# Two transformer blocks on one core: the first block's attention placed between its projection units, and the order in which the split halves of the weights are made

## The chip, the cores and the metric

The kernel runs on one core of one Trainium2 chip. The metric is the device time of one execution in microseconds (us), as the median of three runs. TensorE (PE) multiplies, with its weight loads shown apart as PEld; VectorE (DVE), ScalarE (ACT), GpSimd (POOL) and SyncE (SP) are the other engines. Each of them works through its own list of instructions in order and waits on semaphores for the others.

## The reference, cut to what matters

There are 256 tokens of width 1024. The first block has two layers, the second block one. Everything is float32.

```python
for i in range(2):                                   # first block
    xn = rms_norm(h, norm_mix[i]);  mn = rms_norm(mem, norm_mem[i])
    mk, mv = split(mn @ w_mem_kv[i])                 # 4 memory heads of 64
    proj = xn @ w_in[i]                              # q, k, v of 12 heads of 64; in layer 0 12 forget
                                                     # gates; and the query of the 4 memory heads
    # layer 0: s = q k / 8 + F[t] - F[s], F = cumsum(log_sigmoid(gate)), causal, softmax, p v
    # layer 1: s = q k / 8 - slope * (t - s),        causal, softmax, p v   (256 tokens: one block)
    # memory heads: softmax(qm mk / 8) mv            over 256 memory rows, no mask
    h = h + concat(heads) @ w_out[i]
    gu = rms_norm(h, norm_ffn[i]) @ w_gate_up[i]     # 2 x 2816 columns
    h = h + (silu(gu[:, :2816]) * gu[:, 2816:]) @ w_down[i]
x = rms_norm(h, norm_final)
mod = silu(c) @ w_ada + b_ada                        # 6 x 1024 values, used in the second block
# second block: a latent attention of 8 heads, a gated linear recurrence, and a layer of 16384 experts
# of which each token takes 128 rows of expert_u and 128 of expert_v
```

## The kernel before, in words

**Weights.** The dense weights are a stream of units of 128 x 1024 floats (512 KB). SP loads them two at a time into a ring of six units. One unit is what TensorE needs for one output tile of 128 columns over the whole depth of 1024 (or for half of a 256-column value tile, or for one row block of `w_down`).

**Split products.** In the first block each matmul is made of three products in a faster number format: every operand is split into a high half (rounded) and a low half (the rest), and high x high, low x high and high x low are added. For each unit u, ScalarE copies the raw unit to its high half (`split_hi`, L771), VectorE subtracts it to get the low half (`split_lo`, L1067), and TensorE then runs 8 + 8 + 8 matmuls (`split_T`, L413, L418 and L422; `pair_S`, L449; `down`, L552, L556 and L557). There are three buffers for split units, so the split of unit u waits until unit u-2 has begun on TensorE (`split_begun`). `units_begun` counts the low halves done; TensorE waits for it before the low product, and in `down` before the first product.

**A layer.** In the order of the stream: memory keys (2 units), memory values (2), in layer 0 the forget gates (1), then q (6 units), k (6), v (6), memory queries (2), then the whole attention, then `w_out` (8 units), then the feed-forward (66 units). So layer 0 has 33 units before its feed-forward and layer 1 has 32. Norms are sums of squares by a matmul with ones (L462), a square root on ScalarE (L761), a reciprocal (L1053) and eight scalings (L1059) on VectorE, and then the split of the normed input chunk by chunk (L784, L1080).

**Attention** (`attention`, one for each engine) has 32 items in each layer, an item being one head and one block of 128 queries, with 128 keys for the first block, and 256 for the second and for memory heads. For an item TensorE makes the scores (L489, and in layer 0 another matmul that subtracts F, L493), VectorE masks (L1100 in layer 0, L1103 in layer 1, a copy L1107 for memory heads) and takes the maximum (L1113), ScalarE takes the exponential and its sum (L802), VectorE inverts the sum (L1118) and scales (L1124), TensorE transposes the probabilities (L503), ScalarE copies them (L812), TensorE multiplies by v (L516), and ScalarE stores the head twice (L819, L820). The transposes and the product with v run three and four items behind the scores. These matmuls are plain float32. During attention no weight unit is used.

**Feed-forward.** The units are g0 u0 g1 u1 d0, then g(f) u(f) d(f-1) for f = 2 to 21, then d21, where g is gate, u is up and d is down. TensorE follows that order. VectorE and ScalarE do not split in step with f: both enter the feed-forward with two units split already (by the loop over `w_out`), and VectorE's loop is, for each f from 2:

```python
split_lo(d(f-1)); split_lo(g(f+1)); product(f); split_lo(u(f+1)); product_lo(f); ada_sum(...)
```

`product` (L1167) is silu(gate) x up, which waits until TensorE has finished u(f) (`up_ready`). `product_lo` (L1174) is the low half of it. `ada_sum` (L1152, L1155) is one of the 48 rows of `mod`, whose weights POOL loads into two buffers. One is done for each f in both feed-forward loops, and the 12 that are left between the q and k units of layer 1, with the angles for the second block's rotary embedding (`trig`).

**The second block** starts at about 820 us. From about 1200 us it is the expert layer, whose rows come by indirect DMA.

## Time and profile before

| what | us |
|---|---|
| median of the three runs (1812.03 to 1815.88) | 1815.13 |
| the profiled execution's own time | 1809.4 |
| its span | 1807.7 |
| PE / DVE / ACT busy in the span | 1595.3 / 1018.7 / 726.1 |
| layer 0: from the first q unit to the end of `w_out` | 49.15 to 225.13 |
| of it attention | 108.38 to 200.72 |
| layer 1: the same | 444.62 to 620.99 |
| of it attention | 517.48 to 595.58 |
| feed-forward of layer 0, from g2 on | 250.90 to 425.94 |

The span runs from the first to the last instruction. Busy time is what an engine's instructions took; a matmul counts as busy at either level of TensorE's clock, so a busy TensorE can still run at half speed. "PEclk" is the granted clock as a share of 2.4 GHz: 0.50 is 1.2 GHz.

### The profile page before, as it was taken

What the parts mean: (1) busy time and instruction counts of PE and PEld (TensorE: products, weight loads), DVE (VectorE), ACT (ScalarE), POOL (GpSimd) and SP (SyncE); (2) the same over time, 40 slices, a digit from 0 to 9 for tenths busy, and PEclk for the clock granted to TensorE, in tenths of its full rate; (3) what the DMA queues carried; (4) which work ended last, traced back from release to release, by engine and by line L of the source; (5) the groups of instructions that cost most, each with busy time, mean ns of one, the idle gap of its engine ahead of it and who ended that gap; (6) DMA issues with size and microseconds to landing.
All of it is one profiled execution on the core that took longest, in us unless ns stands there. A gap on an engine that the chain in (4) does not pass through costs nothing.

```text
span 1807.7 us, 23290 instructions
## 1 busy us (share of the span) xinstructions
PE 1595.3 (88%) x7836; PEld 1144.4 (63%) x7836; DVE 1018.7 (56%) x2272; ACT 726.1 (40%) x1750; POOL 513.4 (28%) x573
## 2 busy tenths in 40 slices
PE   5999999999899899997999997888887778777776
PEld 4975789998865799996888786444442223222222
DVE  4443476666654566663335315666666667666644
ACT  4543354444343444443154201434444444444432
POOL 1000000000100000000000001777777776777773
PEclk9975899999975899998999899999999999999999
DMA  7420247664730256662433233999999999999997
GB/s 282 165 92 1 71 152 254 239 249 152 255 118 1 94 198 244 244 220 76 144 110 119 70 140 118 411 410 409 409 409 409 409 409 409 410 409 409 409 410 285
DMA packets 102017, 443.97 MB, mean 246 GB/s; under 512 B 11376, under 2 KB 11648, under 8 KB 84272
## 3 DMA queue, kind: packets, MB, share of 16 engines
q0 software_dynamic: 81632, 297.80, 42.0%
q1 hardware_dynamic: 19584, 141.57, 21.5%
q10 hardware_dynamic: 720, 3.59, 0.5%
q8 instruction: 43, 0.70, 0.2%
q14 instruction: 38, 0.31, 0.0%
HBM read 441.86 MB, written 1.05 MB: 245 GB/s over the span
## 4 chain that ended last, share of the span: by engine, by line
PE 58%; DMA 22%; POOL 9%; DVE 4%; issue 4%; ACT 2%; ACTq 0%; POOLq 0%; DVEq 0%
DMA late<-expert_v,idx 18%; PE PS L400 12%; PE PS L413 7%; PE PS L418 7%; PE PS L422 7%; POOL attn L348 5%; POOL late L356 5%; PE PS L709 4%; PE PS L516 4%; PE PS L489 3%; PE PS L449 3%; PE PS L552 2%; PE PS L556 2%; PE PS L557 2%; DMA attn<-expert_u,idx 2%
## 5 line engine op out<-in xcount | busy, mean ns | idle before, releaser
L709 PE MATMUL PS<-late,wrg 128*128 128x512 f32 x1024 | 500.2, 616 | 130.6 <-DMA late<-expert_v,idx 114.5
L709 PEld LDWEIGHTS PS<-late,wrg 128*128 128x128 f32 x1024 | 177.5, 190 | 439.1 <-DMA late<-expert_v,idx 276.6
L1545 DVE CUSTOM_DVE_ANT_0 attn<-attn,PS 128x1024 f32<-128x1024 f32 x256 | 312.5, 1221 | 238.3 <-DMA attn<-expert_u,idx 238.3
L348 POOL DMA_INDIRECT attn<-expert_u,idx x256 | 241.4, 943 | 380.8 <-DVE idx L1529 300.5
L356 POOL DMA_INDIRECT late<-expert_v,idx x256 | 241.4, 943 | 98.5 <-PE PS L709 54.3
L334 POOL DMA_DIRECT2D ada<-w_ada x46 | 24.4, 530 | 734.2 <-DVE mod L1155 734.2
L1067 DVE TENSOR_TENSOR early_splits<-ring,early_splits 128x1024 fp32r<-128x1024 f32 x132 | 161.6, 1225 | 98.4 <-ACT early_splits L771 92.3
L771 ACT ACTIVATE early_splits<-ring 128x1024 fp32r<-128x1024 f32 x132 | 139.4, 1057 | 150.6 <-PE PS L413 104.2
L400 PE MATMUL PS<-XN,ring 128*128 128x256 f32 x816 | 183.8, 386 | 15.6 <-DVE XN L1376 7.8
L400 PEld LDWEIGHTS PS<-XN,ring 128*128 128x128 f32 x816 | 158.0, 194 | 42.8 <-DVE XN L1376 8.2
L1013 ACT ACTIVATE gel<-dot 128x1 f32<-128x1 f32 x256 | 51.3, 200 | 283.6 <-DVE dot L1545 283.1
L1067 DVE TENSOR_TENSOR late_split<-ring,late_split 128x1024 fp32r<-128x1024 f32 x65 | 79.6, 1224 | 63.8 <-ACT late_split L771 63.6
L1021 ACT ACTIVATE wrg<-con,wts 128x128 f32<-128x128 f32 x256 | 102.7, 401 | 23.5 <-PE PS L709 0.4
L413 PE MATMUL PS<-x_split,early_splits 128*128 128x256 f32 x600 | 92.3, 297 | 17.4 <-ACT x_split L784 10.0
L771 ACT ACTIVATE late_split<-ring 128x1024 fp32r<-128x1024 f32 x65 | 68.6, 1056 | 77.9 <-PE PS L413 41.5
L556 PE MATMUL PS<-product_split,early_splits 128*128 128x256 f32 x344 | 97.2, 283 | 0.0
L552 PE MATMUL PS<-product_split,early_splits 128*128 128x256 f32 x344 | 96.9, 282 | 0.4 <-DVE early_splits L1067 0.4
L557 PE MATMUL PS<-product_split,early_splits 128*128 128x256 f32 x344 | 96.8, 281 | 0.0
L413 PEld LDWEIGHTS PS<-x_split,early_splits 128*128 128x128 f32 x600 | 82.0, 198 | 21.8 <-issue 18.3
L418 PE MATMUL PS<-x_split,early_splits 128*128 128x256 f32 x600 | 88.2, 292 | 0.0
L422 PE MATMUL PS<-x_split,early_splits 128*128 128x256 f32 x600 | 87.2, 290 | 0.0
L418 PEld LDWEIGHTS PS<-x_split,early_splits 128*128 128x128 f32 x600 | 81.2, 201 | 0.2 <-DVE early_splits L1067 0.2
(245 smaller groups left out, 2341.8 us busy)
## 6 DMA issues: line engine op xcount, KB each, us to landing
ring<-wstream SPq DMA_DIRECT2D x134, 1024.0 KB, 4.8
ada<-w_ada POOLq DMA_DIRECT2D x48, 512.0 KB, 3.9
attn<-expert_u,idx POOLq DMA_INDIRECT x256, 17.7
late<-expert_v,idx POOLq DMA_INDIRECT x256, 17.7
con<-const ACTq DMA_DIRECT2D x1, 1168.0 KB, 11.9
MEM<-mem_t ACTq DMA_DIRECT2D x1, 1024.0 KB, 7.7
X<-x_t ACTq DMA_DIRECT2D x1, 1024.0 KB, 9.6
subk<-sub_keys POOLq DMA_DIRECT2D x1, 1024.0 KB, 7.5
```

The costliest lines, as they stand in the source:

```text
L348: gp.indirect_dma_start(UB[i % SLOTS_U], None, expert_u, bass.IndirectOffsetOnAxis(ap=idx[:, n % 3, k:k + 1], axis=0)).then_inc(u_landed[i ...
L356: gp.indirect_dma_start(VB[i % SLOTS_V], None, expert_v, bass.IndirectOffsetOnAxis(ap=idx[:, n % 3, k:k + 1], axis=0)).then_inc(v_landed[i ...
L400: mm = pe.matmul(PS[:, bank, 0:T], w(k), src[:, k, :], start=(k == 0), stop=(k == KC - 1))
L413: mm = pe.matmul(out, hi_of(u)[:, k * P:(k + 1) * P], xh[:, k, :], start=(k == 0), stop=False)
L418: pe.matmul(out, lo_of(u)[:, k * P:(k + 1) * P], xh[:, k, :], start=False, stop=False)
L422: mm = pe.matmul(out, hi_of(u)[:, k * P:(k + 1) * P], xl[:, k, :], start=False, stop=(k == KC - 1))
L552: mm = pe.matmul(out_o, whi, FH[:, par, :], start=first and o % 2 == 0, stop=False, skip_group_check=True)
L556: pe.matmul(out_o, wlo, FH[:, par, :], start=False, stop=False, skip_group_check=True)
L709: mm = pe.matmul(PS[:, 2 * b + g, :], DIAG[:, i % 8, :], VB[i % SLOTS_V][:, g * 512:(g + 1) * 512], start=n % 8 == 0 and k == 0, stop=n % ...
L771: act.activation(hi_of(u), raw(u), ACT.Copy).then_inc(hi_ready, 1)
L1067: ve.tensor_tensor(lo_of(u), raw(u), hi_of(u).bitcast(F32), ALU.subtract).then_inc(units_begun, 1)
L1545: ve.tensor_tensor_reduce(row, row, H2N[n // 8], 1.0, 0.0, ALU.mult, ALU.add, dot[:, n % 2, k:k + 1]).then_inc(dot_ready, 1)
```

## The change

The first block is rebuilt; the second keeps its order. In words:

1. The units of a layer are used in another order: memory queries first, then q, k and v pair by pair. After 16 of the units TensorE does one *group* of attention (two heads of one query block), so that projection units and groups alternate. Three units of `w_out` are begun before the last heads are there, and finished when they are. The raw stream in memory is unchanged: SP loads units one by one (512 KB each) in the new order.
2. Attention works in groups: one maximum, one reciprocal and one copy of the transposed probabilities for two heads, masks and exponentials for each head. Memory heads are not copied: maximum and exponential read the scores where TensorE wrote them. A group's transposes, scores of the next group and product with v are issued at the end of a unit (`attend`).
3. In ScalarE's order `split_hi` of the unit two ahead stands before the exponentials of the group; in VectorE's order `split_lo` stands before the scaling of its probabilities.
4. The norm of x is computed at the start beside that of the memory, and in layer 1 after the first memory unit. `early_table` asks for ScalarE's function tables earlier. After the feed-forward the sums into X start as soon as two columns of `w_down` are done (`down_part`).
5. Both feed-forwards: ScalarE and VectorE start their loop at the first unit that is not split, in another order (below). Two `ada_sum` for each f in layer 0, one for each of the first 12 in layer 1, none between the projections. `trig` moves into the feed-forward of layer 1, and the split of the normed memory for layer 1 to the last two f of layer 0.
6. `w_rg` and `w_ig` are loaded after the second feed-forward.

```diff
+FUSED = (("qm", 0, 0), ("qm", 1, 1), ("q", 0, 1), ("k", 0, 1), ("v", 0, 1), ("v", 1, 0),
+         ("q", 1, 1), ("k", 1, 1), ("q", 2, 1), ("k", 2, 1), ("v", 2, 0), ("v", 3, 0),
+         ("q", 3, 1), ("k", 3, 1), ("q", 4, 1), ("k", 4, 1), ("v", 4, 0), ("v", 5, 0),
+         ("q", 5, 1), ("k", 5, 1), ("wo", 0, 1), ("wo", 1, 1)) + tuple(("wo", c, 0) for c in range(2, KC))
+PAIR_ORDER = (6, 7, 0, 1, 2, 3, 4, 5)
+HELD = 3
...
@@ tensor @@
+            def attend(layer, before, now):
+                if before is not None:
+                    group_turn(layer, before)
+                if now is not None:
+                    group_scores(layer, now)
+                if before is not None:
+                    group_values(layer, before)
...
+                for s, (kind, c, _) in enumerate(FUSED[:-KC]):
+                    u = FUSED_AT[layer] + s
+                    if kind == "v":
+                        pair_half(bank["v", c | 1], u, c % 2, x)
+                    else:
+                        proj(bank[kind, c], u, x, fresh)
...
+                    attend(layer, before, group_at[s])
+                    before = group_at[s]
...
+                for c in range(HELD):
...
+                    out_part(bank["wo", c], u, PAIR_ORDER[:EARLY], first=True, signal=c == 0)
+                    attend(layer, before, group_at[s])
+                    before = group_at[s]
+                pe.wait_ge(heads_lo, base + 14)
+                for c in range(HELD):
+                    out_part(bank["wo", c], out_at + c, PAIR_ORDER[6:7])
+                pe.wait_ge(heads_lo, base + 16)
+                for c in range(HELD):
+                    mm = out_part(bank["wo", c], out_at + c, PAIR_ORDER[7:8], last=True, signal=c > 0)
...
@@ scalar @@
+                for s, (kind, c, _) in enumerate(FUSED[:-KC]):
+                    split_hi(FUSED_AT[layer] + s + 2)
+                    if layer == 0 and s == 0:
+                        forget_gate()
+                    if before is not None:
+                        group_exps(layer, before)
...                 # take(...) of this unit's tile
+                    if before is not None:
+                        group_turned(layer, before)
+                        group_heads(layer, before)
+                    before = group_at[s]
...
             def feed_forward(layer):
-                u = units[0]
-                split_hi(u)
-                split_hi(u + 1)
+                u = LAYER_AT[layer] + PROJ_UNITS[layer]
...
+                split_hi(u + 2)
                 silu(0, 0, False)
+                split_hi(u + 3)
                 product_hi(0, 0, False)
...
+                split_hi(u + 4)
                 silu(1, 1, False)
-                split_hi(u + 4)
                 product_hi(1, 1, False)
                 u += 5
...
@@ vector @@
+                    if before is not None:
+                        group_tops(layer, before)
+                    split_lo(FUSED_AT[layer] + s + 2)
+                    if earlier is not None:
+                        group_low(layer, earlier)
+                    if before is not None:
+                        group_normalise(layer, before)
+                    earlier, before = before, group_at[s]
...
             def feed_forward(layer):
+                def looped(u, i, m):
+                    split_lo(u + 3 * m, i)
+                    split_lo(u + 3 * m + 1, i)
+                    product(i * 2 + (m + 2), m, True)
+                    split_lo(u + 3 * m + 2, i)
+                    product_lo(i * 2 + (m + 2), m, True)
+
-                u = units[0]
-                split_lo(u)
-                split_lo(u + 1)
+                u = LAYER_AT[layer] + PROJ_UNITS[layer]
+                split_lo(u + 2)
                 product(0, 0, False)
+                split_lo(u + 3)
                 product_lo(0, 0, False)
-                split_lo(u + 2)
-                split_lo(u + 3)
...
+                split_lo(u + 4)
                 product(1, 1, False)
-                split_lo(u + 4)
                 product_lo(1, 1, False)
...
                 u += 5
-                with ve.Fori(0, loops) as i:
-                    for m in range(2):
-                        split_lo(u + 3 * m, i)
-                        split_lo(u + 3 * m + 1, i)
-                        product(i * 2 + (m + 2), m, True)
-                        split_lo(u + 3 * m + 2, i)
-                        product_lo(i * 2 + (m + 2), m, True)
-                        ada_sum(j0 + m, m, i, i * 2 + (steps + m))
+                if layer == 0:
+                    with ve.Fori(0, loops) as i:
+                        for m in range(2):
+                            looped(u, i, m)
+                            for a in range(2):
+                                ada_sum(i * 32 + 16 * (m + 1), i * 4 + (steps + 2 * m + a + 1), i * 4 + (2 * m + a), a)
```

Before, `units[0]` is the layer's first feed-forward unit plus two, because two of its units were split already. After the change u is that first unit itself. So in terms of f, the new loop of VectorE (and of ScalarE, with silu in place of product) is:

```python
split_lo(g(f)); split_lo(u(f)); product(f); split_lo(d(f-1)); product_lo(f); ada_sum(...) as said
```

TensorE's feed-forward loop is unchanged: g(f), u(f), d(f-1).

## Rows read from the trace of the kernel before

**Rows 1.** The page: the granted clock in 40 slices of 45 us.
```profile
PEclk9975899999975899998999899999999999999999
```

**Rows 2.** Busy time by stage: stretch, us, busy (count) of PE, PEld, DVE, ACT, POOL; PEclk, DMA share, GB/s.
```profile
22.20:49.15 26.95, 23.59 (x136) 21.68 (x137) 18.67 (x33) 11.80 (x24) 4.99 (x9) 0.84 0.58 223
49.15:108.38 59.23, 57.93 (x485) 57.52 (x483) 26.35 (x24) 30.91 (x44) 0.00 (x0) 1.00 0.51 178
108.38:200.72 92.34, 86.85 (x268) 51.33 (x269) 36.79 (x136) 34.22 (x131) 0.00 (x0) 0.56 0.03 12
200.72:225.13 24.41, 24.41 (x193) 24.41 (x194) 10.98 (x14) 10.63 (x15) 0.00 (x0) 0.93 0.38 130
250.90:425.94 175.04, 174.95 (x1465) 174.77 (x1464) 115.30 (x161) 76.54 (x102) 9.55 (x18) 1.00 0.66 239
425.94:444.62 18.68, 15.36 (x116) 14.55 (x114) 10.40 (x16) 10.17 (x19) 0.00 (x0) 0.99 0.48 169
444.62:517.48 72.86, 64.76 (x481) 62.74 (x481) 50.86 (x108) 29.57 (x45) 6.36 (x12) 0.91 0.59 217
517.48:595.58 78.10, 73.19 (x220) 39.43 (x221) 35.12 (x136) 32.21 (x129) 0.00 (x0) 0.55 0.04 14
595.58:620.99 25.41, 25.41 (x193) 25.41 (x194) 11.11 (x15) 10.62 (x15) 0.00 (x0) 0.89 0.34 125
```

**Rows 3.** The same view in stretches of 4 us.
```profile
196.00:200.00 4.00, 1.34 (x10) 0.82 (x8) 2.15 (x7) 1.17 (x5) 0.00 (x0) 1.00 0.00 0
488.00:492.00 4.00, 1.69 (x15) 1.49 (x13) 1.23 (x2) 0.10 (x1) 0.00 (x0) 0.99 0.34 135
492.00:496.00 4.00, 2.54 (x12) 2.57 (x13) 3.91 (x8) 1.06 (x1) 1.06 (x2) 0.50 0.37 136
```

**Rows 4.** Timeline of TensorE: start, us, engine, line, out<-in, shapes, count.
```profile
86.36 5.92 PE L449 MATMUL PS<-early_splits,x_split 128*128 128x256 f32 x48
...
129.51 1.22 PE L489 MATMUL PS<-attn 64*128 64x256 f32 x2
...
141.19 1.22 PE L489 MATMUL PS<-attn 64*128 64x256 f32 x2
...
1008.24 1.22 PE L486 MATMUL PS<-attn 96*128 96x256 f32 x2
...
1012.90 0.70 PE L486 MATMUL PS<-attn 96*128 96x256 f32 x2
```

**Rows 5.** Costliest groups in layer 0's attention, shapes apart: count | busy, mean ns | idle before.
```profile
L802 ACT ACTIVATE soft<-soft,nmax 128x256 f32<-128x256 f32 x20 | 10.1, 507 | 39.7 <-DVE nmax L1113 39.7
...
L1124 DVE TENSOR_SCALAR soft<-soft,rsum 128x256 f32<-128x256 f32 x20 | 6.9, 345 | 0.1
L802 ACT ACTIVATION_READ_ACCUMULATOR soft<-soft,nmax 128x1 f32 x32 | 6.0, 186 | 0.0
...
L1118 DVE RECIPROCAL rsum<-ssum 128x1 f32<-128x1 f32 x32 | 4.9, 154 | 0.9 <-ACT soft L802 0.9
```

**Rows 6.** Timeline of VectorE and TensorE in layer 0's feed-forward, d0 and f = 2.
```profile
246.58 1.23 DVE L1067 TENSOR_TENSOR early_splits<-ring,early_splits 128x1024 fp32r<-128x1024 f32 x1 [2.98 <-ACT early_splits L771]
247.95 0.36 PE L552 MATMUL PS<-product_split,early_splits 128*128 128x256 f32 x1 [0.35 <-DVE early_splits L1067]
...
256.60 0.28 PE L552 MATMUL PS<-product_split,early_splits 128*128 128x256 f32 x1
257.02 0.42 DVE L1167 TENSOR_TENSOR soft<-soft,PS 128x256 f32<-128x256 f32 x1 [0.67 <-PE PS L422]
258.00 1.23 DVE L1067 TENSOR_TENSOR early_splits<-ring,early_splits 128x1024 fp32r<-128x1024 f32 x1 [0.56 <-ACT early_splits L771]
259.15 0.42 DVE L1174 TENSOR_TENSOR product_split<-soft,product_split 128x256 fp32r<-128x256 f32 x1
259.48 1.22 DVE L1152 CUSTOM_DVE_ANT_0 ada<-ada,late 128x1024 f32<-128x1024 f32 x1
260.95 1.23 DVE L1067 TENSOR_TENSOR early_splits<-ring,early_splits 128x1024 fp32r<-128x1024 f32 x1
```

More of the change, by code:

```diff
@@ new lines, in group_turn @@
+            def group_turn(layer, g):
+                pair, b = groups[g]
+                nk, base = keys_of(pair, b), len(groups) * layer
+                pe.wait_ge(p_ready, base + g + 1)
+                if g >= 1:
+                    pe.wait_ge(pt_copied, base + g)
+                out, probs = halves(6, nk), two(PR, g, nk)
+                for hh in range(2):
+                    for kc in range(nk // P):
+                        mm = pe.transpose(out[:, hh, kc * P:(kc + 1) * P], probs[:, hh, kc * P:(kc + 1) * P], ident)
+                mm.then_inc(pt_ready, 1)
@@ new lines, in group_normalise @@
+            def group_normalise(layer, g):
+                pair, b = groups[g]
+                nk, base = keys_of(pair, b), len(groups) * layer
+                a = 2 * (g % 2)
+                ve.wait_ge(exp_done, base + g + 1)
+                ve.reciprocal(rsum[:, a:a + 2], ssum[:, a:a + 2]).then_inc(vec_step, one(vec_step))
+                ve.wait_ge(vec_step, own(vec_step))
+                probs = two(PR, g, nk)
+                for hh in range(2):
+                    ins = ve.tensor_scalar(probs[:, hh, :], probs[:, hh, :], rsum[:, a + hh:a + hh + 1], None, ALU.mult)
+                ins.then_inc(p_ready, 1)
@@ L1261, in conv @@
+                last = ve.tensor_scalar(dst, dst, float(np.nextafter(np.float32(np.pi), np.float32(0))),
+                                        -float(np.nextafter(np.float32(np.pi), np.float32(0))), ALU.min, ALU.max)
+                if b == NB - 1 and q:
+                    last.then_inc(angle_ready, one(angle_ready))
+                else:
+                    last.then_inc(vec_step, one(vec_step))
+                    ve.wait_ge(vec_step, own(vec_step))
             def conv():
```

872 lines of the change are left out of this document (518 added, 354 removed).

## The prediction

> **What bounds the kernel now.** I read the page's slices first. The granted clock stands at 9 or full nearly everywhere, but sinks to 7, 5 and 8 around 90 to 220 us and again around 520 to 600 us [rows 1]. Busy time by stage, cut at the ends of the projections and of attention, says what these are: in attention TensorE is busy 86.85 of 92.34 us and 73.19 of 78.10 us at a mean clock of 0.56 and 0.55, while DMA moves 12 and 14 GB/s [rows 2]. Outside, the clock is 0.9 to 1.0, and the feed-forward is TensorE back to back: 174.95 of 175.04 us. Its stretch from 250.90 to 425.94 holds 61 units, so one costs 2.87 us; that is the coin of everything below. The first block is bound by TensorE, in attention by TensorE at 1.2 GHz. The other engines are followed only where TensorE waits for them.
>
> **Part 1: attention between units.** In place of two blocks at 1.2 GHz there are 16 groups in each layer, each behind 2.87 us of dense products. Does the clock stay up? In layer 1's projections it was still 0.99 over 4 us with 1.69 us of matmuls, and fell to 0.50 only in the next 4 us [rows 3], when the engine had been idle for more than half of six. A group and its wait leave no such hole, so I take the upper level.
> - *What attention then costs.* At the lower level one pair of heads takes 141.19 - 129.51 = 11.68 us in layer 0. The same pair of matmuls in the second block's attention has 1.22 us while the clock is down and 0.70 once it is up [rows 4], each with a fixed end of a matmul in it, which a run of them pays once. So I take half of the two stages: 46.2 us in layer 0, 39.0 in layer 1. Bounds: 0.57 of it (49 to 52 in a layer of 92), or the bare passes (about 35).
> - *What the new order makes it wait.* Take t = 0 where TensorE begins a unit. The group's probabilities must be scaled before its transposes, which stand behind the unit at 2.87. VectorE's split starts 258.00 - 256.60 = 1.40 us after a unit's first matmul, since ScalarE makes the high half first, and its successor starts 1.15 later [rows 6]: 2.55. A low half of the heads (about 0.3) and one reciprocal (0.154) and two scalings (0.345 each) follow [rows 5]: 3.70, seen by TensorE at 3.8. The two exponentials (2 x (0.507 + 0.186)) behind ScalarE's split end at about 2.8, so they hide behind VectorE's. The copy of the heads ahead of ScalarE's split adds 0.1 to 0.2. The wait is 1.0 us for each of 16 groups; bounds 0 (if the splits come in between) and 2.
> - *Ends.* The first group of layer 0 stands behind the forget gate's functions, about 2 us. At the end the three split buffers are held by units of `w_out`, so the fourth unit's split starts only when the second closes: high half (L771 on the page, 1.06), low half (1.23) and the way there and back (0.4), less 0.7 of the third unit, about 2 us, and some 0.5 for the last group's heads. In layer 1 the copy of two heads' probabilities is waited for in groups with short scores, about 2 us in all.
>
> Layer 0, from the first q unit to the end of `w_out`: now 225.13 - 49.15 = 176.0. Then 28 units x 2.87 = 80.4, + 46.2 + 16 + 2 + 3 = 147.6. **Saved 28 us.** Layer 1: now 620.99 - 444.62 = 176.4 [rows 2], in which 10 us are the `ada_sum` that held up splits and their cold clock (72.86 us to the start of attention, where 20 units are 57.4 and the slow start takes some 4). Then 80.4 + 39.0 + 16 + 2 + 2.5 = 139.9. **Saved 36 us.**
>
> **Part 2: norms and the start.** 22.20 to 49.15 holds five units, 14.4 of 26.95 us [rows 2]. The norm sum of x and its chain leave the path, but the split of the third unit now stands behind VectorE's reciprocal and eight scalings of x, so a new wait comes. I take 5 us saved, between 0 and 10. Between the layers 18.68 - 15.36 = 3.3 us of idle TensorE are covered by a memory unit, and a wait of about 1 comes the same way: 2 saved. Early sums after layer 1's feed-forward: 1 saved. Loads one unit at a time move the same bytes, with at most 2 rows of `mod` beside them for each f: about 2.6 MB in 11 us, 240 GB/s, which is what the stage moves now (239) [rows 2]. `w_rg` and `w_ig` have 90 us to land. Both cost 0.
>
> **Part 3: the feed-forward loops.** Here the step that decides. Before, VectorE did d(f-1) and g(f+1) before `product(f)`; now it does g(f) and u(f) before it and d(f-1) behind it. `product(f)` waits until u(f) is finished, and d(f-1) is TensorE's next unit, which waits for its low half before its first product. So TensorE stands still while VectorE does a product and a split that used to be ahead. Count from T, the end of u(f), which is 256.60 in the trace, where d started at once [rows 6]: `product` at +0.42; the next instruction 0.33 later (as 259.15 to 259.48), +0.75; the split 1.23, +1.98; TensorE sees it 247.95 - 247.81 = 0.14 later, +2.12; a matmul out of a stop costs 0.08 more. **2.2 us for each f from 2 to 21.** In layer 0 two `ada_sum` follow: `product_lo` at +1.90, the sums at +2.23, each 260.95 - 259.48 = 1.47, so the split of g(f+1) is done at +6.40, and seen at +6.54; TensorE would want it after d and the first third of g(f+1), at 2.12 + 2.95 + 0.96 = +6.03. So 0.5 more for 18 of them.
> - Layer 0: 20 x 2.2 + 18 x 0.5 = 53. Layer 1: 44, with one `ada_sum` ending in time. **Added 97 us.** Bounds: 1.6 us each if product and split alone count (65 in all), 3.5 each (140) if ScalarE's order stretches it. Behind `product_lo` there was slack before: DVE was busy 115.30 of 175.04.
>
> Sum on the profiled execution's own time: 1809.4 - 28 - 36 - 5 - 2 - 1 + 97 = 1834.4. The median of the runs lies 5.7 above that execution, so 1840.
>
> **A rule that speaks against Part 1.** Above 196 us the clock is 1.00 although only transposes and products with v ran, which came at the attention's end [rows 3]. The Trainium skill says otherwise (TensorE: Matmul & The Clock Gate, Part 4: PE-mode transpose): "HAM K=8/8 doesn't engage for transpose-mode (it doesn't count as PE-busy the same way)". By that rule a group counts nearly as idle and rival C is what happens; by the row it does not.
>
> **Rivals.**
> - **A. The probabilities are ready in time** (the other side: faster). If ScalarE's and VectorE's splits come early enough that the transposes never wait, 32 us go: 1840 - 32 = 1808, faster by 0.4%. It decides from a wait below 0.2 us a group on. For it: both engines are busy under half of attention now. Against: the split cannot begin before the unit does, and the chain from there is 3.7 against 2.87. Smaller penalties in the feed-forward (its lower bound) lead to the same place.
> - **B. The feed-forward does not stop** (the text is not what I read, or something else orders these splits): 1840 - 97 = 1743, faster by 4%. Against it: TensorE's wait ahead of `down` and VectorE's order are both in the code, and VectorE's `product` waited 0.67 us for TensorE already [rows 6].
> - **C. The clock falls in every group and comes back in every unit.** Then attention keeps its old price (46 + 39 lost), and each unit behind a group pays what `w_out` paid once, 24.41 - 8 x 2.87 = 1.45 us [rows 2], 32 times: 1840 + 85 + 46 = 1971. For it: attention alone sits at 0.50. Against: [rows 3].
>
> **How the numbers follow.** My forecast 0.62, A 0.20, B 0.09, C 0.09. This kernel's three runs lie within 0.2%, so 0.2% (3.6 us) is about what can be told from no change. My case's own range is 1818 to 1865: each wait of Part 1 by half a microsecond is 16 us, each of Part 3 by 0.3 is 12. Reaching into A it goes down to 1800, and up to 1885 for a clock that falls now and then. Faster: B 0.09, most of A 0.16, a tail of mine 0.03, in all 0.28. Within 0.2%: 0.06. Slower: 0.66.
>
> **What would show it.** In the feed-forward, TensorE idle about 2.1 us before every first matmul of L552's kind, released by VectorE's split, and a period of 10.8 us for three units in layer 1 and 11.3 in layer 0, against 8.6 now. In the projections, clock at 1.00, a wait of about 1 us before the transposes released by the scaling, and 148 and 140 us for the stretches. The forecast is wrong if the feed-forward stays back to back, or if the clock by stage there is under 0.8.

## The result

The changed kernel takes 1836.44 us (median of four runs, 1835.53 to 1836.78); the kernel before took 1813.58 beside it (1805.1 to 1815.88). The ratio is 1.0144, with a 95% interval of 1.0122 to 1.0165: slower by 1.4%. The forecast was 1840, in the range 1800 to 1885. The profiled execution's span is 1835.1 us.

I cut every execution at four marks that all kernels have: the first and last matmul of `down` (the group that carries `split_begun`, L552 before and L740 after) in each layer. A view of one source line gives them as "first and last start":

| us | to first `down` | feed-forward 0 | middle | feed-forward 1 | rest |
|---|---|---|---|---|---|
| before | 248.0 | 177.7 | 217.6 | 176.6 | 987.8 |
| predicted change | -33 | +53 | -38 | +44 | -1 |
| after | 203.2 | 243.0 | 170.3 | 229.3 | 989.3 |
| measured change | -44.8 | +65.3 | -47.3 | +52.7 | +1.5 |

"Middle" is the end of feed-forward 0's last unit, the norms and all of layer 1's projections, attention and `w_out`. The signs of the four large changes are as predicted, each of them is larger than predicted, and the errors nearly cancel: 92.1 us saved instead of 71, 118.0 added instead of 97. So the forecast of the total, 4 us off, is closer than its parts, and that is luck.

The same, as the view by stretches of the changed kernel has it (stretch, us, busy time and count of PE, PEld, DVE, ACT, POOL; PEclk, DMA share, GB/s). The first three rows answer to [rows 2]: the start, layer 0 from the first q unit to the end of `w_out`, and layer 1 the same; then the two feed-forwards:

```profile
22.62:46.17 23.55, 20.30 (x120) 18.94 (x121) 19.34 (x37) 11.57 (x24) 3.92 (x7) 0.78 0.65 239
46.17:177.75 131.58, 116.56 (x944) 102.14 (x942) 69.85 (x142) 71.54 (x156) 0.00 (x0) 0.99 0.32 113
...
462.76:591.10 128.34, 112.64 (x894) 98.50 (x892) 67.68 (x139) 69.10 (x152) 0.00 (x0) 0.99 0.33 116
...
203.20:446.20 243.00, 199.07 (x1488) 193.57 (x1487) 139.84 (x225) 81.67 (x112) 19.01 (x36) 0.93 0.62 212
616.50:845.80 229.30, 189.22 (x1487) 185.40 (x1486) 108.74 (x170) 78.32 (x106) 5.29 (x10) 0.96 0.47 165
```

Read it so: layer 0's projections, attention and `w_out` took 176.0 us at clocks of 1.00, 0.56 and 0.93 [rows 2] and now take 131.6 at 0.99. The feed-forward was TensorE back to back, and now has 43.9 idle us (243.00 - 199.07) in layer 0 and 40.1 in layer 1, and its clock is not full.

What ends those waits, in the view of TensorE's waits of the changed kernel (us in all, times, longest); the first two lines are of 184 to 460 us, the others of 46 to 180:

```profile
PE PS L740 <- DVE early_splits L1289: 39.0, 20, 2.0
PE PS L483 <- DVE late_split L1289: 4.9, 10, 0.6
...
PE PS L609 <- DVE soft L1372: 10.0, 15, 1.6
PE PS L622 <- ACT soft L1011: 2.7, 4, 0.7
```

The first line is Part 3 of the prediction: `down` waits 20 times, 1.95 us each, for VectorE's low half. In layer 1 it does so 20 times too, and a 21st time for 0.16 us. The timeline of one f of layer 0 shows the order at work, beside [rows 6]:

```profile
260.26 0.42 DVE L1454 TENSOR_TENSOR soft<-soft,PS 128x256 f32<-128x256 f32 x1 [4.20 <-PE PS L487]
260.60 1.22 DVE L1289 TENSOR_TENSOR early_splits<-ring,early_splits 128x1024 fp32r<-128x1024 f32 x1
...
261.96 0.36 PE L740 MATMUL PS<-product_split,early_splits 128*128 128x256 f32 x1 [1.97 <-DVE early_splits L1289]
262.07 1.22 DVE L1440 CUSTOM_DVE_ANT_0 ada<-ada,late 128x1024 f32<-128x1024 f32 x1
...
263.50 1.22 DVE L1440 CUSTOM_DVE_ANT_0 ada<-ada,late 128x1024 f32<-128x1024 f32 x1
...
264.99 1.23 DVE L1289 TENSOR_TENSOR late_split<-ring,late_split 128x1024 fp32r<-128x1024 f32 x1
```

VectorE had been idle for 4.20 us before `product`: it had the time for the split of d and did not use it, because `product` stood ahead. Then it does both while TensorE stands still. What the prediction did not have is the clock behind such a stop (stretches of 4 us, same kernel, same place):

```profile
258.00:262.00 4.00, 2.03 (x18) 1.86 (x16) 1.74 (x3) 1.86 (x3) 0.00 (x0) 1.00 0.79 299
262.00:266.00 4.00, 4.00 (x21) 4.00 (x22) 3.72 (x8) 1.13 (x2) 0.84 (x2) 0.57 0.56 153
266.00:270.00 4.00, 4.00 (x36) 4.00 (x35) 1.35 (x2) 0.51 (x2) 0.21 (x1) 1.00 0.83 262
```

After the stop the granted clock falls to 1.2 GHz: 21 matmuls in 4 us where the next stretch has 36. It happens in some of the f only: 10 of the 20 in layer 0 and 5 of the 20 in layer 1, counted in stretches of half a microsecond. From 250 to 260 us, behind a stop that ended at 250.36 and with a second one of 0.57 in it, the clock kept the upper level throughout.

### The profile page after: what moved, and what is told of

It reads as the page before. It is cut to its first block, busy times and chain, and to the rows that moved or that the text cites. A ratio compares the mean times of both kernels' runs of the same rounds, so it can differ in the third digit from the quotient of the medians.

```text
span 1835.1 us, 23173 instructions
## 1 busy us (share of the span) xinstructions
PE 1535.4 (84%) x7836; PEld 1114.1 (61%) x7836; DVE 1002.9 (55%) x2208; ACT 721.3 (39%) x1690; POOL 511.2 (28%) x573
## 4 chain that ended last, share of the span: by engine, by line
PE 47%; DMA 24%; DVE 12%; issue 6%; POOL 5%; ACT 5%; DVEq 0%; ACTq 0%; POOLq 0%
DMA late<-expert_v,idx 20%; PE PS L466 11%; PE PS L483 5%; PE PS L487 5%; PE PS L478 5%; PE PS L879 4%; DVE early_splits L1289 4%; DMA attn<-expert_u,idx 3%; POOL attn L416 3%; POOL late L424 3%; PE PS L740 2%; PE PS L745 2%; PE PS L744 2%; DVE late_split L1289 2%; ACT early_splits L945 2%
## 5 line engine op out<-in xcount | busy, mean ns | idle before, releaser
L466 PE MATMUL PS<-XN,ring 128*128 128x256 f32 x816 | 184.0, 386 | 15.6 <-DVE XN L1655 7.8
L740 PE MATMUL PS<-product_split,early_splits 128*128 128x256 f32 x344 | 109.9, 319 | 78.1 <-DVE early_splits L1289 78.1
L945 ACT ACTIVATE early_splits<-ring 128x1024 fp32r<-128x1024 f32 x132 | 138.9, 1053 | 11.2 <-PE PS L740 5.5
L1454 DVE TENSOR_TENSOR soft<-soft,PS 128x256 f32<-128x256 f32 x44 | 18.5, 421 | 214.2 <-PE PS L487 198.9
L740 PEld LDWEIGHTS PS<-product_split,early_splits 128*128 128x128 f32 x344 | 74.8, 217 | 85.2 <-issue 85.2
L1243 ACT ACTIVATE wrg<-con,wts 128x128 f32<-128x128 f32 x256 | 102.8, 401 | 23.8 <-ACT wts L1239 0.7
L745 PE MATMUL PS<-product_split,early_splits 128*128 128x256 f32 x344 | 107.1, 311 | 0.0
L744 PE MATMUL PS<-product_split,early_splits 128*128 128x256 f32 x344 | 106.6, 310 | 0.0
L1097 ACT ACTIVATE soft<-PS 128x256 f32<-128x256 f32 x44 | 17.0, 386 | 214.8 <-PE PS L487 214.8
L1289 DVE TENSOR_TENSOR late_split<-ring,late_split 128x1024 fp32r<-128x1024 f32 x65 | 79.5, 1224 | 28.4 <-ACT late_split L945 25.8
L1239 ACT ACTIVATE wts<-gel,prob 128x1 f32<-128x1 f32 x256 | 75.4, 295 | 9.3
L478 PE MATMUL PS<-x_split,early_splits 128*128 128x256 f32 x504 | 75.1, 291 | 3.4 <-ACT x_split L951 3.3
L744 PEld LDWEIGHTS PS<-product_split,early_splits 128*128 128x128 f32 x344 | 75.4, 219 | 0.0
## 6 DMA issues: line engine op xcount, KB each, us to landing
X<-x_t ACTq DMA_DIRECT2D x1, 1024.0 KB, 10.1
```

Of the source, the lines that this page charges most:

```text
L466: mm = pe.matmul(PS[:, bank, 0:T], w(k), src[:, k, :], start=(k == 0), stop=(k == KC - 1))
L478: mm = pe.matmul(out, hi_of(u)[:, k * P:(k + 1) * P], xh[:, k, :], start=(k == 0), stop=False)
L740: mm = pe.matmul(out_o, whi, FH[:, par, :], start=first and o % 2 == 0, stop=False, skip_group_check=True)
L744: pe.matmul(out_o, wlo, FH[:, par, :], start=False, stop=False, skip_group_check=True)
L745: mm = pe.matmul(out_o, whi, FL[:, par, :], start=False, stop=last, skip_group_check=True)
L945: act.activation(hi_of(u), raw(u), ACT.Copy).then_inc(hi_ready, 1)
```

## The experiments

The kernels ran in three groups of four (e1 to e4, e5 to e8, e9 to e12), each beside runs of the kernel before on the same chip. The chip of the first two groups needed 1873 us for the kernel before, that of the third 1808. The difference lies behind the last `down` (988 us in the first profiles, 1053 to 1064 on this chip, 988 to 991 on that of the third group); the stretches ahead of it that a kernel leaves alone agree between the chips within 3 us. So sizes are read from stretches of the profiled executions, and ratios from the runs.

| us | to first `down` | ff 0 | middle | ff 1 | rest | median | ratio to before (95% interval) |
|---|---|---|---|---|---|---|---|
| e1 early order in both ff | 201.6 | 181.1 | 170.4 | 176.6 | 1058.1 | 1790.51 | 0.954 (0.9498 to 0.9583) |
| e2 before + late order | 250.9 | 230.7 | 216.1 | 227.8 | 1053.5 | 1984.31 | 1.0585 (1.0542 to 1.0628) |
| e3 early order in ff 1 | 200.1 | 243.2 | 170.3 | 176.6 | 1057.2 | 1849.77 | 0.986 (0.9819 to 0.99) |
| e4 e1 + softmax first | 195.2 | 180.7 | 160.1 | 176.6 | 1056.4 | 1770.6 | 0.9447 (0.9404 to 0.9489) |
| e5 e4 + third unit early | 193.3 | 180.4 | 161.2 | 176.6 | 1057.4 | 1770.73 | 0.9446 (0.9411 to 0.9481) |
| e6 scores x4 | 208.6 | 181.5 | 176.8 | 176.6 | 1060.2 | 1802.92 | 0.9612 |
| e7 transposes x6 | 219.2 | 181.3 | 187.9 | 176.6 | 1063.6 | 1829.36 | 0.9752 |
| e8 product with v x6 | 215.5 | 181.4 | 187.0 | 176.6 | 1053.2 | 1816.33 | 0.9697 |
| e9 thin units | 218.4 | 178.3 | 191.0 | 176.6 | 991.4 | 1757.4 (a single run) | |
| e10 one sum in ff 0 | 201.5 | 230.2 | 169.1 | 229.4 | 988.2 | 1820.79 | 1.0077 (1.0056 to 1.0099) |
| e11 changed, again | 203.3 | 243.5 | 171.7 | 230.9 | 987.9 | 1838.1 | 1.0169 (1.0146 to 1.0192) |
| e12 softmax first alone | 195.3 | 242.6 | 159.9 | 229.4 | 987.9 | 1816.71 | 1.0052 (1.0032 to 1.0072) |

e11 is the changed kernel once more, beside the third group. It was expected at 1890 to 1910 us with a ratio of 1.01 to 1.02, on the chip of the first two groups. The ratio came, 1.0169; the time did not, because the third group ran on another chip than the first two.

### e1, e3: the early order back

```diff
 (ScalarE; VectorE the same with split_lo, product, product_lo)
                 split_hi(u + 2)
+                split_hi(u + 3)
                 silu(0, 0, False)
-                split_hi(u + 3)
                 product_hi(0, 0, False)
                 split_hi(u + 4)
+                split_hi(u + 5)
                 silu(1, 1, False)
+                split_hi(u + 6)
                 product_hi(1, 1, False)
-                u += 5
+                u += 7
...              # the loop over f is unchanged; behind it two units fewer are left to split
```

e3 does this in layer 1 alone.

> The changed kernel, but in both feed-forwards VectorE and ScalarE split two units further ahead, as before the change: d(f-1) and the gate unit of f+1 stand ahead of product(f). Theory 1 (this order alone makes TensorE stand still for 2.0 us in each f, and the clock of layer 0 falls only because of that): the waits before `down` vanish, the two feed-forwards fall from 282.9 and 252.9 us to about 220 and 202, and the time is about 1836 - 63 - 51 = 1722. Theory 2 (the second ada_sum of each f in layer 0, 1.43 us on VectorE, is a part of it): layer 0 keeps 10 to 20 us of its 63, 1735 to 1742. Rival (loads one unit at a time, or a late landing, make the stop, and VectorE's split is only its last link): no change within 0.5%, 1827 to 1845.

> The changed kernel with the early order back in layer 1's feed-forward only; layer 0 keeps the late order and two ada_sum in each f. It divides the loss: theory 1 says 252.9 falls to 202 in layer 1 and nothing else moves, 1836 - 51 = 1785. If the stops of layer 0 let it pay for something later (a load or a sum of mod that layer 1 had under cover), it is above 1795.

e1 took 61.9 us out of feed-forward 0 (243.0 to 181.1) and 52.7 out of feed-forward 1, and moved nothing else ahead of the second block. With the second block of the first chip its span would be 1787.8 - 1058.1 + 989.3 = 1719.0, where 1722 was expected. Theory 2 was too high: with two sums in each f, layer 0 keeps only 3.4 us (181.1 against 177.7). The rival, single loads, falls. e3 took out feed-forward 1's share alone, 52.7 (its feed-forward 0 stayed at 243.2 us and a clock of 0.93), so the two are independent. The two stretches of e1:

```profile
201.60:382.70 181.10, 178.90 (x1488) 177.63 (x1487) 141.23 (x224) 80.14 (x111) 19.01 (x36) 1.00 0.82 286
553.10:729.70 176.60, 176.60 (x1487) 176.60 (x1486) 111.00 (x170) 76.65 (x105) 5.28 (x10) 1.00 0.61 214
```

In layer 0 VectorE is busy for 141.23 us in e1 and 139.84 in the changed kernel. Not the amount of its work but its place decides.

### e2: the late order in the kernel before

```diff
 (VectorE; ScalarE the same with split_hi, silu, product_hi)
                 split_lo(u)
+                product(0, 0, False)
                 split_lo(u + 1)
-                product(0, 0, False)
                 product_lo(0, 0, False)
-                split_lo(u + 2)
-                split_lo(u + 3)
...
+                split_lo(u + 2)
                 product(1, 1, False)
-                split_lo(u + 4)
                 product_lo(1, 1, False)
-                u += 5
+                u += 3
...              # behind the loop, two units more are split
```

> The kernel before, with nothing but the late order of splits in the two feed-forwards of VectorE and ScalarE. Theory 1: 40 stops of 2.2 us and no second ada_sum, 1813.6 + 88 + 2 = about 1904; period of an f 10.8 us in both layers. If the clock falls in every second f in layer 0 as in the changed kernel, and that comes from the stops alone, it falls here too and adds some 8: 1912. Rival (the stop needs the single loads or the second sum of the changed kernel): 1810 to 1840.

It added 53.0 us in layer 0 and 51.2 in layer 1, and left the rest of the first block within 3 us:

```profile
250.90:481.60 230.70, 190.56 (x1485) 187.09 (x1486) 112.11 (x159) 79.30 (x104) 9.54 (x18) 0.96 0.50 182
697.70:925.50 227.80, 188.83 (x1488) 185.40 (x1487) 110.05 (x157) 77.21 (x102) 8.48 (x16) 0.96 0.50 180
```

This is the cleanest measure of the stops, since nothing else changed. In layer 1, 227.8 - 176.6 = 51.2 us over 20 stops is 2.56 each, of which 39.0 / 20 = 1.95 is idle and (188.83 - 176.60) / 20 = 0.61 is longer busy time. The starts of `down` divide it further. From one to the next it takes 8.56 us in the kernel before. With a stop it takes 10.76 where the clock stays up, so such a stop costs 2.2 us; where the clock falls it takes 12.26, so a fall costs 1.5 more. The clock falls 5 times in the 20: 20 x 2.2 + 5 x 1.5 = 51.5. For both layers 88 us were expected (and 2 beside them), or 96 if the clock fell in layer 0; it is 104.2, and the clock falls in both, 6 times in layer 0.

### e10: one sum in place of two

```diff
-                ve.tensor_tensor_reduce(w, w, cs, 1.0, 0.0, ALU.mult, ALU.add, adat[:, s:s + 1]).then_inc(vec_step, 1)
+                if bare:    # the second of an f, layer 0
+                    ve.tensor_copy(adat[:, s:s + 1], w[:, 0:1]).then_inc(vec_step, 1)
+                else: ...   # as before
```

> The changed kernel; in layer 0's feed-forward the second of the two ada_sum of each f is a copy of one element (its sum is left out). Asks what the second sum costs there: the stretch from the first `down` to the last is 243.0 us, and 230.7 in the kernel before with the late order, which has one sum. Theory 1 (the second sum delays the next split by 0.6 us in every second f, and with that second stop the clock falls in more of them): 231 us, 12 less; whole time 0.6% under the changed kernel. Rival (single loads make it): 240 to 243.

Feed-forward 0 took 230.2 us, 12.8 less than in the changed kernel (12 expected), and as much as in e2, which has the loads of the kernel before. The whole time is 17.3 us under that of e11, 0.9% instead of the 0.6% expected, since the two stretches beside it are shorter too (1.8 and 2.6 us). The row of the stretch:

```profile
203.20:433.60 230.40, 191.03 (x1490) 187.35 (x1489) 121.12 (x211) 82.14 (x116) 19.09 (x36) 0.96 0.63 224
```

Of the 12.8, 8.0 is TensorE's busy time (199.07 to 191.03), and the wait at L483 falls from 4.9 us in 10 waits to 0.4 in one. The clock falls in 6 of the f instead of 10. So the second stops, half a microsecond each, cost more by the clock that falls in more of the f than by themselves. In e1, with the same second sum but no first stop, feed-forward 0 is only 3.4 us longer than before the change.

### e4, e12: softmax ahead of the splits

```diff
 (ScalarE)
-                    split_hi(FUSED_AT[layer] + s + 2)
                     if before is not None:
                         group_exps(layer, before)
+                    split_hi(FUSED_AT[layer] + s + 2)
 (VectorE)
-                    split_lo(FUSED_AT[layer] + s + 2)
                     if earlier is not None:
                         group_low(layer, earlier)
                     if before is not None:
                         group_normalise(layer, before)
+                    split_lo(FUSED_AT[layer] + s + 2)
```

e4 has it on top of e1, e12 on top of the changed kernel.

> The kernel with the early feed-forward order in both layers, and in the first block the other edit of the change undone too: ScalarE does a group's exponentials ahead of the split of the unit after next, and VectorE the reciprocal and the two scalings ahead of its low half. Theory 1 (the wait of 0.65 us before the transposes of each group comes from the split standing ahead of the softmax, and the split itself has time, since its unit is two units off): the two stretches lose 8 to 10 us each, and the time is 15 to 20 us under that of the kernel with only the early feed-forward order (about 1722): about 1705. Rival (the split is the tighter of the two: behind the softmax it comes too late and TensorE waits for low halves, 0.5 us and more in 28 units of each layer): 15 to 30 us above it, 1740 to 1750.

> The changed kernel with only the softmax ahead of the splits in the first block; the late order of the feed-forwards stays. Undone beside the early feed-forward order, this edit was worth 20 us. Theory 1 (the two edits are independent): 18 to 21 us under the changed kernel on the same chip, and both feed-forwards as there (243 and 229 us). Rival (earlier groups only bring other waits at the end of the block): under 10 us.

e4 lies 19.9 us under e1 (1770.6 against 1790.51), 6.4 of it ahead of the first `down` and 10.3 in the middle; e12 lies 21.4 under e11, beside it, 8.0 and 11.8 in the same places. So the edit brings the same with either order of the feed-forward (18 to 21 us were expected of e12), and in the two stretches no low half comes later than before: the only wait for one there is that of 2.0 us in `w_out`, as in the changed kernel. The waits before the transposes fall from 10.1 us in e1 to 3.9 in e4 in layer 0, and from 9.9 to 2.3 in layer 1. Timelines of a group of layer 0 with 256 keys, first in the changed kernel (the unit began at 96.53):

```profile
97.97 0.49 ACT L1001 ACTIVATE soft<-soft,nmax 128x256 f32<-128x256 f32 x1
98.10 1.23 DVE L1289 TENSOR_TENSOR late_split<-ring,late_split 128x1024 fp32r<-128x1024 f32 x1 [0.20 <-ACT late_split L945]
...
99.64 0.62 DVE L1372 TENSOR_SCALAR soft<-soft,rsum 128x256 f32<-128x256 f32 x2
...
100.31 0.33 PE L609 MATMUL PS<-con,soft 128*128 128x128 f32 x1 [0.66 <-DVE soft L1372]
```

and in e4 (a like group, the unit began at about 91.62):

```profile
94.03 1.04 ACT L945 ACTIVATE late_split<-ring 128x1024 fp32r<-128x1024 f32 x1
94.15 0.17 DVE L1377 RECIPROCAL rsum<-ssum 128x2 f32<-128x2 f32 x1 [0.96 <-ACT soft L1001]
94.35 0.62 DVE L1381 TENSOR_SCALAR soft<-soft,rsum 128x256 f32<-128x256 f32 x2
95.03 0.66 PE L609 MATMUL PS<-con,soft 128*128 128x128 f32 x4 [0.27 <-DVE soft L1381]
95.10 1.23 DVE L1298 TENSOR_TENSOR late_split<-ring,late_split 128x1024 fp32r<-128x1024 f32 x1
```

In this group the wait falls from 0.66 to 0.27 us. The split now stands last, and its unit is two units away.

### e5: the third unit's low half ahead of the scalings of x

```diff
             invert_rms()
+            split_lo(2)      # moved here from first_block
             scale_norm(XN, X, gain("norm_mix0"), RS, normed)
```

> The kernel with both orders undone (splits early in the feed-forward, softmax ahead of the splits in the first block), and at the start the low half of the third unit put between VectorE's reciprocal and the eight scalings of x, instead of behind them. Theory 1 (TensorE's 3.7 us of idle time at 32.4 and the half clock for 4.43 us after it come from that order alone): third unit at 32.7 to 33.0 instead of 36.07 and at the upper level, a new wait of about 1 us before the fourth, 3 us less in all before the first q unit. Rival (XN then comes 1.2 us later and its splits with it, so TensorE waits just as long before the forget gate's unit): within 1 us. In either case the whole time, about 0.2% less, is at the edge of what can be told; the stretch to the first q unit decides.

Timeline of TensorE, e4 and then e5:

```profile
36.07 4.43 PE L509 MATMUL PS<-late_split,mem_split 128*128 128x256 f32 x24 [3.74 <-DVE late_split L1298]
```

```profile
32.91 3.06 PE L509 MATMUL PS<-late_split,mem_split 128*128 128x256 f32 x24
37.16 3.11 PE L509 MATMUL PS<-early_splits,mem_split 128*128 128x256 f32 x24 [1.19 <-DVE early_splits L1298]
```

Theory 1 is right at the start of the kernel: the forget gate's unit starts 3.1 us earlier (40.10 instead of 43.22), with the new wait of 1.19 as expected. Only 1.9 is left at the first `down` (193.3 against 195.2): the norm behind `w_out` waits 3.2 us for X instead of 2.2. The whole time is the same as e4's.

### e6 to e9: what holds the clock in the groups

e6 to e8 repeat a part of each group's matmuls into the same place; the output doesn't change.

```diff
 (e6)
+                for hh, r in enumerate(rows * 3):
+                    pe.matmul(PS[:, 4 + hh % 2, 0:nk], QT[r, pair, b * P:(b + 1) * P], KT[r, pair, 0:nk], start=True, stop=True)
 (e7, in group_turn; e8 the same in group_values)
-                for hh in range(2):
+                for hh in list(range(2)) * 6:
```

e9 has the repeats of e6 and e8, and only the first pass of each of the 20 projection units of a layer.

> The kernel of e5 with each group's q times k matmuls (64 rows of the array) done four times into the same place; the result is unchanged. It asks which part of attention let the clock sink to half before the change (0.56 with TensorE busy 94%). One set takes about 0.54 us for 256 keys and 0.3 for 128 at the upper level, so three more are 32 x 1.35 = 43 us in all. Theory 1 (what holds the clock is that the dense units come in between, whatever the groups do): the two stretches grow by 43 us less the 7 us of waits that the added work covers, clock 0.97 or more. Theory 2 (matmuls over 64 rows keep the clock down): the clock falls in the groups, the stretches' mean goes under 0.85 and they grow by more than 70 us. Theory 3 (transposes do that): as theory 1.

> The kernel of e5 with each group's transposes done six times into the same place; the result is unchanged. One set takes about 0.22 us for 128 keys and 0.45 for 256, so five more are 32 x 1.7 = 54 us. Theory 1 (dense units in between hold the clock): the stretches grow by about 50 us, clock 0.97 or more. Theory 2 (the 64-row matmuls lower it): as theory 1, for transposes use the whole array. Theory 3 (transposes in a row do not count as work for the clock, as the Trainium skill states in TensorE: Matmul & The Clock Gate, Part 4): clock under 0.85 and more than 80 us.

> The kernel of e5 with each group's products of probabilities with v (128 rows, 64 columns of weights) done six times into the same place; the result is unchanged. One set takes about 0.24 us for 128 keys and 0.5 for 256, so five more are 32 x 1.8 = 58 us. Theory 1: the stretches grow by about 55 us at a clock of 0.97 or more. Theory 2, narrowed (it is the half-used array, whether by rows or by columns): clock under 0.85, over 80 us. Theory 3 (transposes): as theory 1.

> The kernel of e5 with q times k done four times and the products with v six times in each group, and of the 20 projection units of each layer only the first pass (high half times high half: 8 of 24 matmuls) left in; the other two passes are left out, so the projections are less exact. A step between two groups is then about 0.96 us of dense matmuls against some 5 of small ones. With dense units of 2.87 us either multiplication of the small work kept the clock at 0.98 to 1.00. Theory 1 in its strong form (the dense unit between groups is what holds the clock): it falls, to 0.6 to 0.85 over 55:130 and 450:520. Rival (small matmuls hold it by themselves as long as TensorE doesn't stop, and before the change it sank because of the short stops of attention): 0.95 or more, with steps of about 5.9 us.

In e6 the two stretches grew by 15.3 + 15.6 = 31 us against e5 (expected 36), in e7 by 25.9 + 26.7 = 53 (50), in e8 by 22.2 + 25.8 = 48 (55). The stretch 46 to 190 us of e6, e7 and e8:

```profile
46.00:190.00 144.00, 133.52 (x1125) 118.74 (x1124) 71.02 (x142) 68.78 (x155) 0.00 (x0) 0.98 0.30 106
```

```profile
46.00:190.00 144.00, 135.02 (x1137) 122.47 (x1136) 66.38 (x136) 65.82 (x149) 0.00 (x0) 0.99 0.28 93
```

```profile
46.00:190.00 144.00, 138.08 (x1426) 126.54 (x1426) 69.23 (x138) 65.97 (x151) 0.00 (x0) 0.99 0.30 99
```

No kind of attention matmul, repeated alone, pulls the clock down beside dense units: theories 2 and 3 fall as stated. Then e9 took two thirds of the dense work away, and theory 1 in its strong form falls too:

```profile
55.00:130.00 75.00, 62.59 (x723) 53.47 (x724) 35.65 (x74) 30.86 (x77) 0.00 (x0) 0.98 0.28 92
420.00:500.00 80.00, 65.52 (x706) 54.82 (x706) 36.70 (x80) 33.82 (x87) 0.00 (x0) 0.94 0.30 99
...
86.00:87.00 1.00, 0.29 (x2) 0.97 0.79 315
87.00:88.00 1.00, 1.00 (x6) 0.50 0.04 16
...
90.00:91.00 1.00, 1.00 (x10) 0.83 0.59 225
91.00:92.00 1.00, 1.00 (x20) 1.00 0.02 8
```

(The rows of 1 us are of TensorE alone.) Expected was 0.6 to 0.85; it is 0.98 and 0.94. Where it falls, at 87, TensorE had stood still for 1.84 us before, and it is back at about 90.8. What ran in between, from 87.10 on, are small matmuls of the group alone, q times k over 64 rows first of all:

```profile
87.10 2.93 PE L595 MATMUL PS<-attn 64*128 64x256 f32 x12
89.82 0.86 PE L598 MATMUL PS<-attn 64*128 64x256 f32 x4
```

So no dense pass is needed to bring the clock back. In the kernel before the clock fell in the same way, at the start of layer 0's attention behind waits of 0.5 to 1.6 us for the softmax, and stayed down for some 80 us:

```profile
104.00:108.00 4.00, 3.77 (x32) 1.00 0.22 86
108.00:112.00 4.00, 2.43 (x16) 1.00 0.73 262
112.00:116.00 4.00, 3.09 (x10) 0.63 0.00 0
116.00:120.00 4.00, 4.00 (x13) 0.50 0.00 0
...
192.00:196.00 4.00, 4.00 (x19) 0.63 0.00 0
```

There too it came back without a dense unit, at about 195, when no scores were left and only transposes and products with v ran. The rival is right that the clock falls behind a stop. But short stops don't explain why it stayed down. Attention before was idle for 6% of the stretch, at its two ends: from 116 to 192 every 4 us have 4.00 busy ones at 0.50. e9 was idle for 17% and recovered. What is left as a difference is the stream at the lower level. In 4 us there were 11 to 16 matmuls while it stayed down, and 22 in e9 (87 to 91), where the repeats stand behind each other. The number alone does not decide, since there were also only 16 in the last 4 us before it rose (191 to 195). Which property of the stream brings the clock back stays open; runs that vary it alone were not made.

## Why the prediction came out right

By its steps:

- **Part 3, the feed-forward stops: right in mechanism, place, count and price; the clock behind them is missing.** There are 20 stops in each layer, released by VectorE's split. e1, e2 and e3 show that the order alone makes them. One costs 2.2 us where the clock stays up, as predicted (10.76 us from one `down` to the next in layer 1; 10.8 predicted). What the sum lacked are the falls of the clock, 1.5 us each. With them the mean from one `down` to the next is 11.1 us in layer 1 and 11.9 in layer 0, where 10.8 and 11.3 were predicted, and a stop costs 2.56 in the mean of e2. "A clock that falls now and then" was kept for the end of the range and not put in the sum. The trace before had a sign of it. Part 1 reads [rows 3] as a fall behind more than half of 6 us without work; in stretches of half a microsecond TensorE stops at 489.7 and the clock is down at 492.0, some 2.2 us into the stop. Part 3 predicted stops of just that length.
- **The second sum in layer 0: right in cause, too small.** 18 x 0.5 = 9 was predicted, 12.8 measured (e10). Only some 4.5 of it is idle time, half of what was predicted, since there is no second stop in an f where the clock fell (10 waits, not 18); 8.0 is longer busy time.
- **Part 1, the clock: right.** The groups run at 0.99, so rival C (0.09) fell. My reason for it, that a group leaves no such hole, fits, since the waits there are 1.7 us at most; that dense units are needed is not shown (e9).
- **Part 1, what attention costs: mis-sized.** I took half of the old stage, 46.2 us. It is 116.56 - 80.4 = 36.2 in layer 0 and 112.64 - 80.4 = 32.2 in layer 1 (39.0 predicted): close to my lower bound, "the bare passes (about 35)". The two stretches took 131.6 and 128.3 us instead of 147.6 and 139.9. Part of the error is that I halved the whole stage, 92.34 us with its 5.5 idle ones, and then added the waits once more; half of the busy time would have been 43.4. The same matmuls, old and new, in the costliest groups of the two kernels, old first:

```profile
L489 PE MATMUL PS<-attn 64*128 64x256 f32 (+1 forms) x64 | 31.7, 603 | 1.1 <-DVE mid L1329 0.6 <-DVE soft L1100 0.5
L516 PE MATMUL PS<-soft,attn 128*64 128x128 f32 x104 | 29.1, 421 | 0.0
L503 PE MATMUL PS<-con,soft 128*128 128x128 f32 x52 | 18.9, 442 | 1.6 <-DVE soft L1124 1.6
```

```profile
L590 PE MATMUL PS<-attn 64*128 64x256 f32 (+1 forms) x64 | 10.0, 388 | 0.0
L622 PE MATMUL PS<-soft,attn 128*64 128x128 f32 x104 | 9.3, 288 | 3.0 <-ACT soft L1011 2.7
L609 PE MATMUL PS<-con,soft 128*128 128x128 f32 x52 | 9.2, 289 | 10.0 <-DVE soft L1372 10.0
```

  Counts are equal, and q times k and the products with v fall to less than a third, not to half. Halving leaves out that a group puts two heads' matmuls behind each other, so the end of one lies beside the next: 64 x 388 ns is 24.8 us and took 10.0, while 64 x 603 ns is 38.6 and took 31.7. I had written that a run pays its end once, and then did not count with it. That the grouping does this, and not the dense unit beside it, is read from these rows; no run separates the two.
- **Part 1, the waits: chain right, price a third too high.** Transposes start 100.31 - 96.53 = 3.78 after the unit's first matmul; 3.8 was predicted. But the unit takes 3.12 there (to 99.65), since it starts under the group's last products, not the dense 2.87, so the wait is 0.66 and not 1.0: 10.0 us in layer 0 instead of 16. Idle time of the stretch is 131.58 - 116.56 = 15.0 instead of 21. Rival A needed 0.2. The wait of about 2 us at the fourth unit of `w_out` is there with 2.0. That the wait before the transposes comes from the split's place is shown by e4 and e12, which take most of it away.
- **Part 2:** 3.0 us at the start (49.15 to 46.17) instead of 5, 2.5 between the layers (18.68 to 16.21) instead of 2, both with the new wait as said (3.1 and 1.0 us). A loss that no term had lies between the end of `w_out` and the first `down`: 25.5 us instead of 22.9 in layer 0, 25.4 instead of 22.3 in layer 1. TensorE now waits 2.2 and 2.5 us there for X (L522, released by VectorE), which it did not before; why X comes later was not studied.

By its parts, then, the sum was 21 us short on each side, and that 1840 came so near to 1836 is luck. The direction hung on it too: with the savings as measured and the additions as priced, the time would have been about 1836 - 21 = 1815, no change from the kernel before.

Rival B, the feed-forward that does not stop, is e1. It was priced at 97 us and is worth 114.6.

The rule weighed against Part 1 (the Trainium skill, TensorE: Matmul & The Clock Gate, Part 4: PE-mode transpose) says that transposes do not count as busy for the clock in the same way. With six times the transposes e7 stands at 0.99. Beside dense units that neither needs the rule nor refutes it. The row set against the rule holds: in the kernel before the clock rose at about 195, when no other matmuls than transposes and products with v had run since 191.5; these two were never run apart. The prediction stretched the rule from transposes to the whole group, and the rival of 131 us that it backed did not come.

Both edits named in the change go the wrong way: late splits in the feed-forwards cost 114.6 us, splits ahead of the softmax some 20. With both orders undone the rebuilt block is worth 1873.42 - 1770.6 = 102.8 us, 5.5%, on the chip of e4. e4 and e5 beat both kernels (ratios 0.9447 and 0.9446 to the kernel before; the changed kernel has 1.0144 and 1.0169).

## What to carry to other kernels

An operation that only prepares something for the bottleneck needs the right place in its engine's order. If the bottleneck's next step needs it, it must stand ahead of any operation that waits for the bottleneck. If its own user is two steps off, it must stand behind the operation whose result the bottleneck needs sooner. So ask of each operation not when it can run, but who waits for it first. A stop of the bottleneck costs its length and then what the clock does after it: here 2.2 us, and 1.5 more in the 5 to 10 of 20 cases in which the clock fell. And when work is priced from a row at the other clock level, count also what the new neighbours change: two heads' matmuls in one run cost less than a third of what they did apart at half the clock.

## What the runs showed of the hardware

- In late-order feed-forwards the granted clock falls to 1.2 GHz behind a stop of 1.97 us in 5 or 6 of 20 f and not in the others (e2, e10, layer 1 of the changed kernel), and the mean is 0.96. With a second stop of up to 0.57 it falls in 10 of 20, and the mean is 0.93 (layer 0 of the changed kernel).
- Attention before stood at 0.50 for some 80 us, with TensorE busy 4.00 of every 4.00 us from 116 to 192; small matmuls alone brought the clock back in e9 within 4 us, and at its end in the kernel before.
- Chips differ. The same second block took 989 us on one and 1058 on another, at clocks of 0.97 and 0.93, the changed kernel and e1 (988 in e11, the changed kernel again on the chip of the third group):

```profile
845.80:1835.10 989.30, 832.38 (x2543) 457.54 (x2541) 550.48 (x1404) 366.47 (x1057) 482.78 (x516) 0.97 0.79 310
```

```profile
729.70:1787.80 1058.10, 834.59 (x2543) 467.75 (x2541) 549.04 (x1404) 360.42 (x1057) 483.36 (x516) 0.93 0.77 290
```

  DMA moved 310 and 290 GB/s. TensorE's busy time is nearly equal (832.38 and 834.59 us), so most of the 69 us is idle time; what makes it was not studied.
